# Eight row chunks of the second modulation all summed on VectorE, the silu of their condition behind the second norm, more filler products, another order of the row splits

## The reference

```
mod = c @ w_mod + b_mod                      # 6 x 1024: sh1, sc1, gt1, sh2, sc2, gt2   (block 2: silu(c) @ w_ada + b_ada)
h   = rmsnorm(x, g) * (1 + sc1) + sh1
y   = mixers(h)                              # block 1: causal pooling and forgetting attention; block 2: two attentions
x   = x + gt1 * (y @ w_out)
h2  = rmsnorm(x, g2) * (1 + sc2) + sh2
q   = h2 @ w_query                           # 8 heads x 2 x 128
top 16 of 128 keys per half, top 16 of the 16 x 16 pairs, gate = softmax
x   = x + gt2 * sum(gate * gelu(h2 . u[e]) * v[e])     # 16384 experts e, 128 chosen per token
```

## Time and profile before

| | |
|---|---|
| median of 3 runs | 1972.68 us (1967.51 to 1976.87) |
| profiled execution: time, span | 1963.73 us, 1961.9 us |
| TensorE busy | 1893.8 us (97%) |
| VectorE busy | 1622.2 us (83%) |
| ScalarE busy | 1085.0 us (55%) |
| GpSimd busy | 568.2 us (29%) |
| mean granted clock of TensorE | 0.992 of 2.4 GHz |
| HBM traffic | 276 GB/s over the span |

### The profile page before, as it was taken

One profiled execution on the slowest core, in us unless ns is written; L12 is line 12 of the kernel. 1 busy time (PEld: TensorE's weight loads), 2 busy tenths in 40 slices (PEclk: granted clock), 3 DMA queues, 4 the chain that ended last, 5 costly groups with the idle time before them and its releaser, 6 DMA issues.

```text
span 1961.9 us, 36055 instructions
## 1 busy us (share of the span) xinstructions
PE 1893.8 (97%) x13546; PEld 1841.5 (94%) x13546; DVE 1622.2 (83%) x3384; ACT 1085.0 (55%) x2128; POOL 568.2 (29%) x498
## 2 busy tenths in 40 slices
PE   7999889999999999999999999999999999999997
PEld 5998889999999999999999988999999999999997
DVE  3777768889899989889777775588888998898997
ACT  3345555644566665555556554465445665555554
POOL 0000221444533234445200000034354332444351
PEclk8999999999999999999999999999999999999999
DMA  8764667678699899999856672566887898999995
GB/s 345 271 236 162 254 210 228 226 271 310 242 319 317 303 358 360 347 347 356 321 204 203 252 252 79 169 213 218 285 290 267 316 319 298 343 356 345 361 337 194
DMA packets 143469, 543.85 MB, mean 277 GB/s; under 512 B 15744, under 2 KB 16128, under 8 KB 138432
## 3 DMA queue, kind: packets, MB, share of 16 engines
q1 hardware_dynamic: 99312, 363.38, 52.7%
q0 software_dynamic: 40608, 160.06, 22.5%
q10 hardware_dynamic: 3376, 18.11, 2.5%
HBM read 539.78 MB, written 1.05 MB: 276 GB/s over the span
## 4 chain that ended last, share of the span: by engine, by line
PE 66%; DVE 13%; DMA 9%; issue 6%; ACT 5%; POOL 1%; SPq 0%; ACTq 0%; DVEq 0%; POOLq 0%
PE PB L1021 16%; PE PB L997 14%; PE PB L1022 7%; DVE WL L1813 5%; DMA RING<-in_v 5%; PE PB L994 4%; PE PB L959 4%; PE PB L586 4%; PE PB L587 4%; PE PB L588 4%; DMA RING<-in_u 3%; ACT WH L1324 2%; PE PB L992 2%; PE PB L908 2%; DVE AR L1838 1%
## 5 line engine op out<-in xcount | busy, mean ns | idle before, releaser
L1813 DVE TENSOR_TENSOR WL<-RING,WH 128x1024 fp32r<-128x1024 f32 x517 | 640.0, 1240 | 194.1 <-ACT WH L1324 190.1
L1324 ACT ACTIVATE WH<-RING 128x1024 fp32r<-128x1024 f32 x517 | 545.4, 1056 | 446.2 <-DMA RING<-in_v 161.2
L1021 PE MATMUL PB<-HX,WH 128*128 128x384 f32 x2048 | 587.7, 360 | 8.0 <-DVE WL L1813 7.4
L1022 PE MATMUL PB<-HX,WL 128*128 128x192 f32 x2048 | 512.7, 250 | 0.0
L1021 PEld LDWEIGHTS PB<-HX,WH 128*128 128x128 f32 x2048 | 384.5, 188 | 12.3 <-issue 11.7
L1022 PEld LDWEIGHTS PB<-HX,WL 128*128 128x128 f32 x2048 | 391.1, 191 | 0.0
L997 PE MATMUL PB<-AR,RING 128*128 128x192 f32 x2144 | 372.1, 326 | 0.0
L997 PEld LDWEIGHTS PB<-AR,RING 128*128 128x128 f32 x2144 | 348.1, 190 | 0.0
L2571 POOL DMA_INDIRECT AR<-in_v,SPX x128 | 244.6, 1911 | 320.8 <-DVE AR L2284 268.1
L994 PE MATMUL PB<-HX,WH 128*128 128x384 f32 x854 | 254.1, 361 | 0.0
L992 PE MATMUL PB<-HX,WL 128*128 128x192 f32 x976 | 227.8, 254 | 0.0
(11 more groups left out here) (277 smaller groups left out, 2891.2 us busy)
## 6 DMA issues: line engine op xcount, KB each, us to landing
RING<-in_u SPq DMA_DIRECT2D x256, 512.0 KB
RING<-in_v SPq DMA_DIRECT2D x256, 512.0 KB
RING<-in_win SPq DMA_DIRECT2D x90, 512.0 KB
AR<-in_wr POOLq DMA_DIRECT2D x24, 1024.0 KB, 5.4
RING<-in_wq SPq DMA_DIRECT2D x32, 512.0 KB
AR<-in_wr ACTq DMA_DIRECT2D x12, 1024.0 KB, 6.6
AR<-in_wm SPq DMA_DIRECT2D x8, 1024.0 KB, 16.4
RING<-in_wout SPq DMA_DIRECT2D x16, 512.0 KB
```

Source lines behind the costliest of these rows:

```text
L1021: e.matmul(both_parts(c), hi(n_v + n)[:, cs], dense(k), start=start, stop=False)
L1022: return e.matmul(PB[c][:, 0:T], lo(n_v + n)[:, cs], HH[:, k, 0:T], start=False, stop=stop)
L1324: e.activation(hi(t), raw(("w", t), words(t)), ACT.Copy).then_inc(s_hi, 1)
L1813: e.tensor_tensor(lo(t), raw(("w", t), words(t)), hi(t).bitcast(F32), ALU.subtract).then_inc(s_lo, 1)
```

## The change

It does the following.

- All of chunks 24 to 31 are summed by VectorE's `row_sum`: 24 to 27 in the query tiles 7, 9, 11 and 13, and 28 to 31 in the up tiles 1, 4, 7, 10, 13, 16, 19 and 22, half a chunk in each (`ROW_AT`). GpSimd's products and ScalarE's sums of them go.
- `choice_turns` counts each half chunk with 130 units and spreads the sum of both kinds over the 82 tiles. The plan is the same for both blocks. With it the 57 steps of half 0 end in up tile 44 instead of 40, and `PK` is written in tile 45 instead of 41; those of half 1 end in tile 81 instead of 80. VectorE makes 22 of the adds of a block and GpSimd 39, where it was 27 and 34. `DOT_AT` stays as it was.
- The silu of `CRX` moves from the start of the output projection to behind `norm_mod(1)` and the fills of the first query tiles.
- GpSimd's queue loads 24 and 25 at the same place as before, 26 and 27 after `columns`, and 29, 30, 28, 31 as chunks 24, 25, 26, 27 have been summed.
- ScalarE's order in `norm_mod` 1 to 3 becomes turned, high, turned, high.
- Fillers: 10 behind the first transposes; 4 each before the third and fifth step of the first half of `pool_in` 0; 12 instead of 8 ahead of the second norm's square root; 3 behind `columns`; 3 each at `s_bt` 14 and 15 in block 2.

```diff
+NEXT_SLOT = {24: 1, 25: 2, 26: 0, 27: 3, 28: 0, 29: 1, 30: 2, 31: 3}
+ROW_AT = {1 + 3 * i: (28 + i // 2, i % 2) for i in range(8)}
-N_PROD = 4
-NEXT_SLOT = {24: 1, 25: 2, 26: 1, 27: 2, 28: 0, 29: 3, 30: 1, 31: 2}
...
     for j in range(NK):
-        share, count = sum(work) * min(j + 1, JG - 2) / (JG - 2), 0
+        rows = 130 * sum(i <= j for i in ROW_AT)
+        share, count = (sum(work) + 130 * len(ROW_AT)) * min(j + 1, JG - 2) / (JG - 2) - rows, 0
...
# TensorE
                     for k in range(4):
                         kk = 4 * u + k
+                        if (c, a) == (0, 0) and kk in (2, 4):
+                            busy(2 if kk == 2 else 3, 4)
...
             transposed(0)
+            busy(3, 10)
...
             busy(6, 3)
-            for n in (7, 8):
-                e.wait_ge(s_xu, n)
-                busy(6, 2)
+            e.wait_ge(s_xu, 7)
+            busy(6, 3)
+            e.wait_ge(s_xu, 8)
+            busy(6, 4)
             e.wait_ge(s_sq, 9)
-            busy(6, 1)
+            busy(6, 2)
...
             for g in range(20, 24):
                 columns(g)
+            busy(3, 3)
...
+            for n in (14, 15):
+                e.wait_ge(s_bt, n)
+                busy(1, 3)
             e.wait_ge(s_bt, 16)
...
# ScalarE
-                turned(0)
-                turned(1)
-                high(0)
-                turned(2)
-                high(1)
-                turned(3)
-                high(2)
-                high(3)
+                for kp in range(4):
+                    turned(kp)
+                    high(kp)
...
-            e.wait_ge(s_crx, 16)
-            e.activation(CRX, CRX, ACT.Silu).then_inc(s_silu, 1)
             sqrt_table()
-            def product_sum(g):
-                e.wait_ge(s_prod, g - 23)
-                for j in range(2):
-                    w, c = row_chunk(g)[:, j, :], 2 * g + j
-                    r = e.activation(w, w, ACT.Copy, accum_out=MC[:, c:c + 1])
-                r.then_inc(s_msum, 1)
...
             norm_mod(1, 0, 24, 8)
             fill(W_WQ)
             fill(W_WQ + 1)
+            e.wait_ge(s_crx, 16)
+            e.activation(CRX, CRX, ACT.Silu).then_inc(s_silu, 1)
...
-                            if blk == 0 and t in (6, 8):
-                                product_sum(23 + t // 2)
...
# VectorE
                             if blk == 0 and t in (7, 9, 11, 13):
-                                row_sum(28 + (t - 7) // 2, 0)
-                                row_sum(28 + (t - 7) // 2, 1)
+                                row_sum(24 + (t - 7) // 2, 0)
+                                row_sum(24 + (t - 7) // 2, 1)
...
+                    if blk == 0 and j in ROW_AT:
+                        row_sum(*ROW_AT[j])
                     for _ in range(choose_steps(j)):
...
# GpSimd
-            def products(g):
-                e.wait_ge(*chunk_landed(g))
-                for j in range(2):
-                    w = row_chunk(g)[:, j, :]
-                    r = e.tensor_tensor(w, w, CRX, ALU.mult)
-                r.then_inc(s_prod, 1)
             load(24)
             load(25)
-            e.wait_ge(s_silu, 1)
-            products(24)
-            products(25)
-            for g in (26, 27):
-                e.wait_ge(s_msum, g - 25)
-                load(g)
-            products(26)
-            products(27)
             e.wait_ge(s_mcol, nth(24))
-            load(28)
-            load(29)
-            for g in (30, 31):
-                e.wait_ge(s_msum, g - 27)
+            load(26)
+            load(27)
+            for g, done in ((29, 1), (30, 2), (28, 3), (31, 4)):
+                e.wait_ge(s_mdv, done)
                 load(g)
```

More of the change, by code:

```diff
@@ L54 @@
 N_TILES = 651
+N_EARLY = 8
+N_MID = 8
+NEXT_SLOT = {24: 1, 25: 2, 26: 0, 27: 3, 28: 0, 29: 1, 30: 2, 31: 3}
+ROW_AT = {1 + 3 * i: (28 + i // 2, i % 2) for i in range(8)}
 EARLY = 12
@@ L76 @@
 ROW_LAND = {g: sum(ROW_SLOT[h] == s for h in ROW_SLOT if h <= g) for g, s in ROW_SLOT.items()}
-N_EARLY = 8
-N_MID = 8
-N_PROD = 4
-NEXT_SLOT = {24: 1, 25: 2, 26: 1, 27: 2, 28: 0, 29: 3, 30: 1, 31: 2}
-NEXT_LAND = {g: sum(NEXT_SLOT[h] == NEXT_SLOT[g] for h in NEXT_SLOT if h <= g) for g in NEXT_SLOT}
-def summed_before(g):
-    return g - 24 - N_PROD
 OUT_ORDER = [(0, 0), (1, 0), (0, 1), (1, 1), (2, 0), (2, 1), (3, 0), (3, 1)]
@@ L306, in two_block_kernel @@
         s_crx, s_next = sem("s_crx"), [sem(f"s_next{i}") for i in range(4)]
-        s_prod, s_msum = sem("s_prod"), sem("s_msum")
         s_sq, s_ms, s_rt, s_xn = sem("s_sq"), sem("s_ms"), sem("s_rt"), sem("s_xn")
@@ L496, in chunk_landed @@
             if g >= 24:
-                return s_next[NEXT_SLOT[g]], 16 * NEXT_LAND[g]
+                return s_next[NEXT_SLOT[g]], 16 * (1 + g // 28)
             return s_chunk[ROW_SLOT[g]], 16 * ROW_LAND[g]
@@ L1780, in scalar_program @@
                     e.wait_ge(s_used, W2_GATE + u + 1)
-                    e.wait_ge(s_mdv, summed_before(24 + N_EARLY + N_MID))
+                    e.wait_ge(s_mdv, N_EARLY + N_MID)
                     for p, dst in ((i - 1, gsT), (i, gdT)):
@@ L1834, in row_sum @@
                     e.wait_ge(s_cr, 16)
-                if (g, j) in ((24 + N_PROD, 0), (24 + N_EARLY, 0)):
-                    e.wait_ge(s_silu, 1 if g < 24 + N_EARLY else 2)
+                if (g, j) in ((24, 0), (24 + N_EARLY, 0)):
+                    e.wait_ge(s_silu, 1 if g == 24 else 2)
                 by = CRX if 24 <= g < 24 + N_EARLY else CR[g // 24]
@@ L2331, in peer @@
                     if blk == 0 and n == 12:
-                        e.wait_ge(s_mdv, N_EARLY - N_PROD)
-                        e.wait_ge(s_msum, N_PROD)
+                        e.wait_ge(s_mdv, N_EARLY)
                         add_rows(48, 48 + 2 * N_EARLY, C_B2, 2)
@@ L2526, in vector_program @@
             fill(W2_GATE + 16)
-            e.wait_ge(s_mdv, summed_before(48))
+            e.wait_ge(s_mdv, 24)
             add_rows(48 + 2 * N_EARLY, 96, C_B2 + 2 * N_EARLY, 1)
@@ L2655, in gpsimd_program @@
                 if g < 24 + N_EARLY + N_MID:
-                    e.wait_ge(s_mdv, summed_before(max(24 + N_EARLY, g - 1)))
+                    e.wait_ge(s_mdv, max(N_EARLY, g - 25))
                 else:
-                    e.wait_ge(s_mdv, summed_before(g))
+                    e.wait_ge(s_mdv, g - 24)
                     e.wait_ge(s_ps, 4)
```

2 lines of the change are left out of this document (removed).

## The result

The changed kernel takes 1990.11 us (median of 6 runs, 1978.60 to 2002.34); the kernel before, timed beside it, 1973.83 (6 runs, 1967.51 to 1976.87). These medians lie 16.3 us apart. The ratio of the comparison is 1.010, with a 95% interval of 1.0075 to 1.0126: about 20 us slower (15 to 25), where I had forecast 4 us less. The time lies above my range (to 1979).

A forecast was written before the change was run, and what follows sets the result against it. TensorE, busy 97%, was taken as the bound. Terms -6.1 - 4.8 + 0.7 - 0.3 - 0.3 + 0.5 - 0.4 + 7.0 gave about -4 us, 1968.7 us on the median; range 1957 to 1979.

The forecast's parts named there:

- What bounds the kernel: Whole kernel: TensorE busy 97%, so a change pays only where TensorE stands still or runs at its lower clock.
- Output tiles, -6.1: Last six output tiles: removing GpSimd's products and the early silu closes two holes and a lower-clock stretch, -6.1 us.
- Norm, -4.8: Second norm and first query tile: the 4.01 us operation falls to 0.17, the stage ends earlier, -4.8 us.
- the +0.7 for the clock: Second norm: allowance in case the lower clock returns there all the same, up to 3 us; +0.7 booked.
- Start -0.3: Start of the kernel: new fillers cost time but may hold the clock; between -2 and +2.5 us, -0.3 taken.
- Row sums and plan, +7.0: Up tiles: eight half-chunk sums and the new choice plan cost 3.5 us per block, +7.0 in both.
- demand 95.4, room 91.7: VectorE, tiles 46 to 82: 80.9 busy, 4 added, 7 wait, 3.5 fixed waits against 91.7; +3.5 us per block.
- The wait in tile 46: Up tile 46: with PK four tiles later, VectorE waits about 7 us (3 to 10) for the first gather.
- The denser plan: Up tiles 46 to 82: the shared plan adds about 4 us of VectorE work per block.
- little changes there: Up tiles 0 to 23: the plan moves 7.3 us of choice out against 10.4 us of sums in block 1.
- VectorE in tile 46 decides: Rival, up tiles: nothing of wait and added work is absorbed, 11 us per block, +11, 1983.7 us; chance 0.12.
- The late gathers are hidden: Rival, tile 46: the 7 us for late gathers fall away, -11, 1961.7 us; chance 0.27.
- The fillers cost and do not hold the clock: Rival, start, norm and block 2: fillers make it about 6 us worse, +2, 1974.7 us; chance 0.13.

The follow-up runs named there:

- experiment 5: Changed kernel with the silu back at its old place ahead of the output tiles; 1989.53 us in one run.
- after: The changed kernel as described, against the kernel before; 1990.11 us, ratio 1.010.
- the second profile of before: The kernel before, unchanged, profiled once more; 1971.43 us, span 1969.6.
- experiment 3: Kernel before with only the changed planner's line, without the half chunks it makes room for; 1992.30 us, ratio 1.0136.
- experiment 6: Kernel before with the changed planner's line and the first twelve dot products of each block four up tiles later; 1979.15 us, ratio 1.0042.
- experiment 7: Kernel before, its plan kept, with the first twelve dot products of each block four up tiles later; 1970.74 us, ratio 1.0012.
- experiment 11: Changed kernel with old planner's line, the eight chunk sums in queries and first 14 up tiles, and the fillers of before; 1962.89 us, ratio 0.9966.
- experiment 2: Changed kernel with the planner's line of before, so PK is written in tile 41 again; 1971.10 us, ratio 1.0005.
- experiment 4: Changed kernel without the row sums of chunks 28 to 31, a two-column copy standing in for each; 1987.57 us, ratio 1.0101.
- experiment 9: Changed kernel with old planner's line, six chunks summed by VectorE in the queries and two in four up tiles; 1967.53 us, ratio 0.9978.
- experiment 1: Changed kernel with the first twelve dot products of each block four up tiles later; 1978.95 us, ratio 1.0053 against the kernel before.
- experiment 8: Changed kernel with old planner's line and without the row sums of chunks 28 to 31; 1968.35 us, ratio 0.9990.

## Why the prediction was wrong, point by point

**What bounds the kernel: right in kind.** The places named were the places that moved. What the prediction did not see is how little of VectorE's idle time is free in the tiles 38 to 82.

**Output tiles, -6.1: 4.0 measured.** GpSimd's hole and the lower clock went as worked out (though 18 products in 3.41 us for 2.1 make 1.3 us of clock, not 1.5, and experiment 5 shows that the hole ahead does not explain the fall alone). The 2.15 us of the silu did not. The step that failed is "I see no wait for it", said of the landing of the last output tile; it now sets the end (experiment 5). Two chunks on GpSimd's queue and two on ScalarE's are issued 15.1 to 16.1 us behind the broadcast, before and after. They and the weights share the DMA engines, which were full. With the silu moved, the last tile's load is issued 2.3 us earlier (19.8 us behind the broadcast, not 22.1), but it is there to be rounded at 31.5 us with either place of the silu.

**Norm, -4.8: right; the +0.7 for the clock did not come.** From E to the end of the stretch at the norm it is 18.3 us (239.3 to 257.6) against 23.4 before (244.1 to 267.5), 5.1 less; the second profile of before has 25.0 there, the three of experiments 3, 6 and 7 have 22.8 to 23.0. The transposes begin where the fillers were to put them, and the clock held. By the Trainium skill (TensorE: Matmul & The Clock Gate, PE-mode transpose), transposes do not count as busy in the same way as other products, and the clock could have fallen behind them. It did so in experiment 11, behind 3.8 us of transposes and one-column products and a wait of 0.49; in after, with fillers around the same work, it did not.

**Silu behind the norm 0, queries -0.3: right** (queries 0.5 us shorter). **Start -0.3:** more likely about +1. The seven profiles with the new fillers reach the broadcast at 202.2 to 203.3 us, 202.6 in the mean, the seven with the old ones at 200.1 to 203.2, 201.6 in the mean. The lower level of the clock lasts 6.8 or 10.2 us in all in the start with the new fillers and 10.2 or 13.6 with the old ones, so they cost more than they gave back. **Norm order +0.5, block 2 fillers -0.4:** below what the traces resolve. The slow stretch around 1192 is there in three of the seven profiles with the old fillers and in none of the seven with the new ones.

**Row sums and plan, +7.0: wrong, and this decided.** The step was "demand 95.4, room 91.7" (whose difference is 3.7 and not the 3.5 booked). It had three parts.

- *The wait in tile 46.* Its mechanism and size were right: 7 us written, 7.08 measured in block 1 and 6.93 in block 2. Counted from the scores in tile 38, the first gather goes out at 28.8 us (424.8 less 396.0), where it went out at 18.1; 28.1 was written. The landing took 6.1 us to the start of the dot product, where I had taken 5, and VectorE came to the dot product 1.4 us later than before: two errors that nearly cancel.
- *The denser plan.* 4 us of work written, 3.8 measured, and 3.6 of them as time (experiment 7).
- *The idle time that was to absorb both.* This failed. I took 5.3 of 8.8 us of idle VectorE over 37 tiles, plus 2 us that TensorE was ahead, as room for a wait that stands at the beginning of them. TensorE can live only on the splits it has in hand at that moment; then it stood for 5.96 us. And it came back at half the clock for 4.3 us of its busy time, so 2.1 us more. Of these 8.1 us the rest of the stage won back some 2 (below). Nor did idle time absorb the denser plan. VectorE's idle time in the tiles 38 to 82 (length less busy) is 16.3 to 18.5 us in the four blocks of before, 17.1 to 19.0 in the four of the new plan with later dots, and 19.1 in both of experiment 2. It is 22 to 25 only where the gather is late (after, experiments 3, 4 and 5). Its work changed and its idle time did not: these 16 to 19 us were no reserve.

So per block: 3.6 for the plan, and for the wait with its clock 129.1 - 119.5 - 3.6 = 6.0 us (129.1 is after's mean). The split takes for granted that the two add up. Together 9.6 us where I had 3.5: 19 instead of 7.

**Tiles 0 to 37, "little changes there": wrong by 4 us.** Here too there is a floor: VectorE's idle time in block 1 is 11.0 us in both profiles of before, 10.2 in after, 11.3 in experiment 2, 9.3 in experiment 9. What lies above the floor could be used: in experiment 4, with the new plan and no sums, it is 17.1 us, and of the 9.8 us that the sums put on top in after, 6.9 came out of it and 2.8 became time. The new plan frees 5 to 6 us of VectorE's work there (76.5 busy in block 2 against 82.0), which bring nothing in block 2 (93.9 us for 94.8). The row sums put some 10 on top in block 1; six of the eight in the up tiles took 1.55 to 1.62 us instead of 1.21 to 1.22, 2.3 us in all, for which I had booked nothing. It does save 5.3 us against the old plan with the same sums (98.0 for 103.3), and pays 19 for it later.

**The rivals.** What came is "VectorE in tile 46 decides", which I gave 0.12: 11 us per block with nothing absorbed, against 9.6 measured. Its argument against, "the 8.8 us of idle time", was the one that should have been dropped. Chance and range suffered from the same step, since the forecast's range ended where that rival begins. "The late gathers are hidden" falls by experiment 1. "The fillers cost and do not hold the clock" is half right: they cost (about 1 us in the start, 0.9 at the norm), but they hold the clock at the norm.

**One reading of the prediction is wrong.** It takes the 2.17 and the 4.01 us as agreeing with a lock between operations with two SBUF inputs and GpSimd's. The additions of 2.17 us (`X<-X,AR`) have two inputs; the operation of 4.01 us (`ST<-ST`) has one. It ended at 251.68 us, and the second of the two products of GpSimd that ran beside it at 251.65.

**What stays open.** The stretches of the two up loops are 22.4 us longer than in the mean of before's two profiles, 9.8 us come back at the norm, and the spans differ by 11 us (1976.8 against 1965.8), while the medians differ by 16 and the ratio says 15 to 25. Runs of after scatter over 24 us, and its only profile is the lowest. Experiment 5, which differs from it by the silu alone, has 131.3 and 130.4 us in the tiles 38 to 82 and a lower clock (0.97) in tiles 0 to 37 too, 1987.7 in all. That fits the median of after, but one profile does not settle it. Open too is why experiment 8 shows so little of its gain: 9.8 us in the stretch, 2.0 by the ratio, with -2.8 to +6.7 as the interval; 9 and 11, with more work in the up tiles, show 4.3 and 6.7.

## What to carry to other kernels

When an engine that splits tiles for the bound engine stands still for longer than its lead, the bound engine stands too, and here the tiles that followed won back only 2 of 8 us: count the lead in tiles at the place where the wait stands, and do not average idle time over the tiles that follow. Idle time can have a floor that added work does not use up; two versions with different work show where it lies. A planner's line that is shared between two loops is paid in both; look at the tile in which its last result comes out, and at which order of a transfer and its consumer hangs on that tile. When a change removes a hole, look for the transfer that lands next before the hole is booked as gained.

## What the runs showed of the hardware

- Waits of TensorE of 4.3 to 6.8 us in the middle of steady up tiles (5.96 and 5.80 in after, 4.31 and 5.83 in experiment 3, 6.15 and 5.80 in experiment 4, 5.80 and 6.83 in experiment 5) went with 6.8 us at 0.50 of the clock each time. Of the six waits of 1.9 to 2.4 us in experiments 1, 6 and 7, four were followed by 3.4 us at 0.50, while the mean clock of the tiles 38 to 82 stayed at 0.99 to 1.00.
- A VectorE operation on two numbers per row took 4.01 us in both profiles of before while GpSimd multiplied, and 0.15 to 0.17 us at all five places in after, where the products are gone. In both it ended 0.04 us or less behind the second of the two products that ran beside it.
- With the DMA share at 1.00 and four 1 MB chunks under way, a 512 KB weight tile was issued 19.8 us behind the broadcast in after and could be rounded at 31.5, and ScalarE stood 3.0 to 3.1 us for it (after, experiment 5).
